# Opening of a two-layer diffusion step: a third input unit in PSUM banks of its own, its products spread between the modulation chunks

## What is computed

```python
def modulation(cond, w, b):
    m = jax.nn.silu(cond) @ w + b
    return m.reshape(cond.shape[0], 1, N_MOD, D_MODEL)

def modulate_in(x, g_pre, mod, j):
    return rmsnorm(x, g_pre) * (1.0 + mod[:, :, 3 * j + 1]) + mod[:, :, 3 * j]

def swiglu(h, w13, w2):
    a, g = jnp.split(h @ w13, 2, axis=-1)
    return (jax.nn.silu(g) * a) @ w2
```

## Time and profile before

| | us |
|---|---|
| runs | 2427.45, 2427.62, 2428.94 (median 2427.62) |
| the profiled execution | 2429.22 |
| its span | 2427.4 |
| busy: PE, DVE, ACT, POOL | 2392.8 (99%), 1747.2, 981.5, 435.0 |
| PE busy from 20 to 30, 30 to 40, 40 to 50 us | 5.09, 8.06, 8.86 |
| PE busy from 50 to 60, 60 to 70 us | 9.88, 10.00 |

### The profile page before, as it was taken

The page is one execution under the profiler, slowest core; times in us unless marked ns, Lnnn a source line. Parts: engine busy times, 40 slices in busy tenths (PEclk is TensorE's granted clock), DMA queues, the critical chain, the costliest instruction groups (busy, mean ns, idle before and its releaser), DMA issues. The chain is left out here.

```text
span 2427.4 us, 38749 instructions
## 1 busy us (share of the span) xinstructions
PE 2392.8 (99%) x15053; PEld 2196.1 (90%) x15053; DVE 1747.2 (72%) x2469; ACT 981.5 (40%) x1917; POOL 435.0 (18%) x462
## 2 busy tenths in 40 slices
PE   7999999999999999999999999999999999999998
PEld 6998999899889799979988997999899989989997
DVE  5988786566554779778846978885677769856863
ACT  4442343533445455324434442453511154423432
POOL 2220121211114223102213210220300021201211
PEclk9999999999999999999999999999999999999999
DMA  7526333385122453353253426334254433243333
GB/s 232 164 62 217 96 87 117 117 265 161 50 60 74 116 176 87 126 162 87 79 182 108 120 70 230 92 87 133 69 165 151 128 122 96 62 148 96 88 115 112
DMA packets 347227, 297.94 MB, mean 123 GB/s; under 512 B 38798, under 2 KB 296838, under 8 KB 347046
## 3 DMA queue, kind: packets, MB, share of 16 engines
q1 hardware_dynamic: 341798, 278.64, 38.1%
q0 software_dynamic: 5248, 16.83, 1.9%
HBM read 280.57 MB, written 14.80 MB: 122 GB/s over the span
## 5 line engine op out<-in xcount | busy, mean ns | idle before, releaser
L2071 DVE TENSOR_TENSOR w_lo<-w_raw,w_hi 128x512 fp32r<-128x512 f32 (+1 forms) x243 | 204.5, 845 | 225.4 <-ACT w_hi L1456 224.2
L1456 ACT ACTIVATE w_hi<-w_raw 128x512 fp32r<-128x512 f32 (+1 forms) x243 | 181.5, 752 | 445.2 <-DMA w_raw<-in_ffn_w_dram 202.5
L942 PE MATMUL psum<-w_hi,act_hi 128*128 128x512 f32 x800 | 318.3, 398 | 0.4 <-DVE w_lo L2071 0.4
L944 PE MATMUL psum<-w_hi,act_lo 128*128 128x512 f32 x800 | 317.1, 396 | 0.0
L943 PE MATMUL psum<-w_lo,act_hi 128*128 128x512 f32 x800 | 317.0, 396 | 0.0
L1080 PE MATMUL psum<-hT_hi,w_hi 128*128 128x320 f32 x912 | 281.9, 309 | 0.9 <-DVE z_quarters L2376 0.9
L1081 PE MATMUL psum<-hT_lo,w_hi 128*128 128x320 f32 x912 | 281.8, 309 | 0.0
L1082 PE MATMUL psum<-hT_hi,w_lo 128*128 128x320 f32 x912 | 281.8, 309 | 0.0
L1977 POOL TENSOR_TENSOR w_sum<-w_raw 128x512 f32<-128x512 f32 x36 | 54.8, 1523 | 744.0 <-DVE w_lo L2338 744.0
L1080 PE MATMUL psum<-t_hi,w_hi_more 128*128 128x320 f32 x608 | 187.9, 309 | 0.0
L1082 PE MATMUL psum<-t_hi,w_lo_more 128*128 128x320 f32 x608 | 187.9, 309 | 0.0
(11 more groups left out here) (319 smaller groups left out, 6003.1 us busy)
## 6 DMA issues: line engine op xcount, KB each, us to landing
w_raw<-in_ffn_w_dram SPq DMA_DIRECT2D x92, 512.0 KB, 5.1
w_raw_next<-in_ffn_w_dram SPq DMA_DIRECT2D x80, 512.0 KB, 5.3
w_raw<-in_ffn_w_dram SPq DMA_DIRECT2D x148, 256.0 KB, 3.2
ada_tile_ffn<-in_ada_w_dram SPq DMA_DIRECT2D x56, 512.0 KB, 4.1
ada_direct<-in_ada_w_dram POOLq DMA_DIRECT2D x32, 512.0 KB, 6.0
w_raw<-in_ab_w_in_dram SPq DMA_DIRECT2D x27, 512.0 KB, 4.0
ada_tile_sc<-in_ada_w_dram SPq DMA_DIRECT2D x24, 512.0 KB, 3.7
w_raw<-in_sc_w_in_dram SPq DMA_DIRECT2D x23, 512.0 KB, 4.0
```

The source lines that it names most:

```text
L942: mm(out, a_hi, b_hi, start=first, stop=False)
L944: return mm(out, a_lo, b_hi, start=False, stop=final)
L1456: A(dst, src, ACT.Copy).then_inc(w_hi_ok, 1)
L2071: V.tensor_tensor(d_, a, b.bitcast(F32), ALU.subtract).then_inc(w_lo_ok, 1)
```

## The change

The third unit (unit 2) gets banks 6 and 7; the columns of the modulation move from bank 7 into the upper half of banks 4 and 5. Unit 2's block is requested behind the second chunk. Its split stands ahead of chunk 1's rows on ACT and DVE. PE's order is rewritten, the opening doing all three units. DVE and ACT take the k steps one at a time. Behind the opening, DVE's split of unit 3 stands ahead of the split of u, and POOL's two sums wait for `w_lo_ok` 4 in the first sublayer, the low part of unit 3.

```diff
         THIRD = pair(6)
+        FIRST_COLS = 256
...
+                if c_ == 1:
+                    dma(next_raw[:], ffn_w13[0, 0].rearrange("(k p) n -> p k n", p=P)[:, :, FF + P:FF + 2 * P]).then_inc(next_loaded, 16)
-            dma(next_raw[:], ffn_w13[0, 0].rearrange("(k p) n -> p k n", p=P)[:, :, FF + P:FF + 2 * P]).then_inc(next_loaded, 16)
...
-                    last = nc.tensor.transpose(PS[:, 7, col:col + 2], mrow0[:, c_, i, :], ident[0:2, 0:2])
+                    last = nc.tensor.transpose(PS[:, 4 + c_ % 2, col:col + 2], mrow0[:, c_, i, :], ident[0:2, 0:2])
...
-                    for k in range(CK):
-                        for r in range(2):
-                            products(r, k)
-                    for c_ in range(1, CHUNKS):
-                        first_modulation(c_)
-                        if c_ == 1:
-                            first_columns(1)
-                            continue
-                        for j in range(CK):
-                            for r in range(2):
-                                products(r, (c_ - 1) * CK + j)
-                            if j == 0:
-                                first_columns(c_)
+                    both(0)
+                    both(1)
+                    first_modulation(1)
+                    products(2, 0)
+                    first_columns(1)
+                    products(2, 1)
+                    first_modulation(2)
+                    both(2)
+                    first_columns(2)
+                    both(3)
+                    first_modulation(3)
+                    products(0, 4)
+                    first_columns(3)
+                    products(1, 4)
+                    both(5)
+                    products(2, 2)
                     for r in range(2):
                         for k in range(KD - CK, KD):
                             products(r, k)
+                    for k in range(3, KD):
+                        products(2, k)
...   direct_step
-                    if s > 1:
+                    if s != 1:
                         pe.wait_ge(in_evac[UB[s] % 2], inv(plan[s][0], UB[s]) + 1)
...   the loop over units behind the opening
-                            for r in range(1 if s and i == 1 else 0, 2):
+                            for r in range(1 if i == 1 else 0, 2):
...   ACT, opening: split of unit 1 between k 0 and 1, unit 2 behind k 1
+                    modulate_first(c_ * CK)
+                    if c_ == 0:
+                        split(plan[0][0]["nin"] + 1)
+                    modulate_first(c_ * CK + 1)
+                    if c_ == 0:
+                        act.wait_ge(next_loaded, 16)
+                        A(next_hi[:], next_raw[:], ACT.Copy).then_inc(w_hi_ok, 1)
...   POOL
-                    pool.wait_ge(w_lo_ok, plan[s][0]["nin"] + 3)
+                    pool.wait_ge(w_lo_ok, plan[s][0]["nin"] + (3 if s else 4))
...   DVE, opening
+                first_rows(0)
+                first_cols(0)
+                split(n)
+                split_first(0)
+                split(n + 1)
+                split_first(1)
+                dve.wait_ge(w_hi_ok, n + 3)
                 V.tensor_tensor(next_lo[:], next_raw[:], next_hi[:].bitcast(F32), ALU.subtract).then_inc(w_lo_ok, 1)
+                first_rows(1)
+                first_cols(1)
+                split_first(2)
+                first_rows(2)
+                split_first(3)
+                first_cols(2)
+                split_first(4)
+                first_rows(3)
+                split_first(5)
+                first_cols(3)
+                split_first(6)
+                split_first(7)
...   DVE, mixed_in
-                    if i and not (s and i == 1):
+                    if i > 1:
                         split(nb + 1 + 2 * i)
...
-                    if s and i == 0 and ph["plain"]:
+                    if i == 0 and ph["plain"]:
                         split(nb + 3)
                     split_act(i, act_hi[:, i, :], act_lo[:, i, :], ut[:])
```

More of the change, by code:

```diff
@@ L920, in first_columns @@
                 for i in range(2 * CK):
-                    col = (i // CK * KD + c_ * CK + i % CK) * 2
-                    last = nc.tensor.transpose(PS[:, 7, col:col + 2], mrow0[:, c_, i, :], ident[0:2, 0:2])
+                    col = FIRST_COLS + (i // CK * KD + c_ * CK + i % CK) * 2
+                    last = nc.tensor.transpose(PS[:, 4 + c_ % 2, col:col + 2], mrow0[:, c_, i, :], ident[0:2, 0:2])
                 last.then_inc(mod_mm, 1)
@@ L982, in products, with both @@
                             pe.wait_ge(w_lo_ok, n + 1)
-                        for a, b in ((w_hi, hT_hi), (w_hi, hT_lo), (w_lo, hT_hi)):
+                        hi, lo = (next_hi, next_lo) if r == 2 else (w_hi[:, n % 2], w_lo[:, n % 2])
+                        out = THIRD if r == 2 else IN[n % 2]
+                        for a, b in ((hi, hT_hi), (hi, hT_lo), (lo, hT_hi)):
                             for h in range(2):
-                                last = mm(IN[n % 2][:, h, 0:HT], a[:, n % 2, k, :], b[:, k, h * HT:(h + 1) * HT],
-                                          start=(k == 0 and a is w_hi and b is hT_hi), stop=(k == KD - 1 and a is w_lo))
+                                last = mm(out[:, h, 0:HT], a[:, k, :], b[:, k, h * HT:(h + 1) * HT],
+                                          start=(k == 0 and a is hi and b is hT_hi), stop=(k == KD - 1 and a is lo))
                         if k == KD - 1:
                             last.then_inc(pe_unit, 1)
-                    for k in range(CK):
-                        for r in range(2):
-                            products(r, k)
-                    for c_ in range(1, CHUNKS):
-                        first_modulation(c_)
-                        if c_ == 1:
-                            first_columns(1)
-                            continue
-                        for j in range(CK):
-                            for r in range(2):
-                                products(r, (c_ - 1) * CK + j)
-                            if j == 0:
-                                first_columns(c_)
+                    def both(k):
+                        products(0, k)
+                        products(1, k)
+                    both(0)
[14 more added lines that the diff above has]
+                    products(2, 2)
                     for r in range(2):
@@ L1030, in in_unit @@
                 for k in range(KD):
-                    hi, lo = (next_hi[:, k, :], next_lo[:, k, :]) if ph["nin"] == 0 and first(r) and i == 1 else (w_hi[:, p, k, 0:width], w_lo[:, p, k, 0:width])
+                    hi, lo = w_hi[:, p, k, 0:width], w_lo[:, p, k, 0:width]
                     for a, b in ((hi, hT_hi), (hi, hT_lo), (lo, hT_hi)):
@@ L1514, in opening, with modulate_first @@
                     A(h_mod[:, :, q * P:(q + 1) * P], TR(0, q), ACT.Copy).then_inc(kept_by_act, 1)
+                def modulate_first(k):
+                    for cd, tok in ((0, slice(0, LAT)), (1, slice(LAT, TOK))):
+                        last = A(h_mod[:, k, tok], h_mod[:, k, tok], ACT.Identity, scale=mcol[:, 0, 1, cd, k:k + 1], bias=mcol[:, 0, 0, cd, k:k + 1])
+                    last.then_inc(first_hmod, 1)
                 for c_ in range(CHUNKS):
@@ L1520, in opening @@
                         split(plan[0][0]["nin"])
-                        split(plan[0][0]["nin"] + 1)
                         act.wait_ge(x_kept_dve, 3)
@@ L1658, in mixed_in @@
                     need(act, in_evac[(nb + 1) % 2], inv(ph, nb + 1) - 1 + i)
-                    A(halves(sg[:]), THIRD_V if s and i == 1 else IN_V[nb % 2], ACT.Silu).then_inc(in_evac[nb % 2], 1)
+                    A(halves(sg[:]), THIRD_V if i == 1 else IN_V[nb % 2], ACT.Silu).then_inc(in_evac[nb % 2], 1)
                     if i == 1:
@@ L2150, in evac, with split_first @@
                     V.tensor_copy(dst, src).then_inc(out_evac, 1)
[L2152 to L2157, removed]
+            def split_first(k):
+                dve.wait_ge(first_hmod, k + 1)
+                own.link(V.tensor_copy(hT_hi[:, k, :], h_mod[:, k, :]))
+                V.tensor_tensor(hT_lo[:, k, :], h_mod[:, k, :], hT_hi[:, k, :].bitcast(F32), ALU.subtract).then_inc(first_hT, 1)
             def opening():
@@ L2174, in opening, with first_rows @@
                 n = plan[0][0]["nin"]
[L2175 to L2178, removed]
+                def first_rows(c_):
                     dve.wait_ge(mod_mm, 2 * c_ + 1)
@@ L2181, in opening, with first_cols @@
                         V.tensor_copy(mrow0[:, c_, i, :], PS[32 * i:32 * i + 2, 4 + c_ % 2, 0:P]).then_inc(first_row, 1)
+                def first_cols(c_):
+                    ks = slice(c_ * CK, (c_ + 1) * CK)
                     dve.wait_ge(mod_mm, 2 * c_ + 2)
-                    turned_ = PS[:, 7, 0:4 * KD].rearrange("p (a k c) -> p a k c", a=2, c=2)
+                    turned_ = PS[:, 4 + c_ % 2, FIRST_COLS:FIRST_COLS + 4 * KD].rearrange("p (a k c) -> p a k c", a=2, c=2)
```

(6 more changed lines are left out.)

## The result

| | us |
|---|---|
| before, 21 runs | 2428.94 median (2427.08 to 2431.61) |
| changed, 21 runs | 2432.94 median (2430.97 to 2437.87) |
| ratio | 1.0018, 95% interval 1.0012 to 1.0024 (+2.9 to +5.8 us) |
| changed again, beside other kernels | 1.0013 (1.0004 to 1.0022), twice |
| profiled execution of the changed kernel | 2431.89, span 2430.1 |

One of the 33 runs of the kernel before that stand beside the first four experiments took 4005.03 us at a mean granted clock of 0.616, against 0.997 to 0.999 in the others; it is left out everywhere.

A forecast was written before the change was run, and what follows sets the result against it. PE was taken as the bound, busy 2392.8 of 2427.4 us. The opening's 3.3 us gain is eaten by the wait for POOL's direct loads, net +1.0 on 2427.62: 2428.6 us, range 2424.0 to 2432.2.

The forecast's parts named there:

- POOL's gate: POOL's sums start 3.6 us later, so the direct loads land late; PE stands some 4 us, unit 4 +1.0 us.
- the delay of POOL: POOL's sums beside DVE's copy and subtraction of u: delay bounded by 0 and 1.3 us, taken as 0.
- the clock: PE's new stand from 64.4 is broken by the direct steps, longest piece about 1.9 us: no fall forecast.
- the base: The kernel before's median, 2427.62 us, onto which the forecast difference was put.
- The loads, the start, unit 1's end: Opening: unit 2's block at 30.0, chunk 2 at 36.0, chunk 3 at 42.0; first pair done 0.65 us earlier.
- PE at unit 3 3.3 us earlier: Five k steps of unit 2 remain after the first pair, ending at 57.3 instead of 60.61.
- the cover of other steps: DVE's later work, such as unit 4's `w_lo` at 67.5, ends before PE needs it at 71.1: hidden.
- The 72.4: Start of unit 4 in us if DVE goes first with both its operations, blocking POOL.
- Rival B: Clock falls in PE's stand at the direct steps: 2.9 to 3.4 us on top of +1.0, 2431.8 us; chance 12%.
- Rival A: The gain stays: direct loads land before PE waits much, unit 4 at 66.8; -3.3 us, 2424.3 us; chance 20%.
- Rival C: Opening does not shrink, unit 2's early split standing ahead of chunk 1's rows; +1.6 us, 2429.2 us; chance 8%.
- Its sign: Rival C's mark in the profile: the last product of unit 1 not before 53.6 us.

The follow-up runs named there:

- the first four experiments: Four of the follow-up runs, timed beside 33 runs of the kernel before; the text does not say which four.
- filled: Changed kernel plus 14 further matmuls ahead of the first direct step, filling PE's wait; run twice, 2433.16 and 2433.47 us, ratio 1.0015 to before.
- gate 4 alone: Kernel before with only POOL's two sums in the first sublayer moved to wait for unit 3's low part; 2432.63 us, ratio 1.0013.
- early loads: Changed kernel, bias and first four direct loads issued after four k steps of h, sums gated by unit 2's low part; 2426.95 and 2428.75 us, 0.9991.
- gate 3: Changed kernel with POOL's sums waiting for unit 2's low part again, as before; 2428.72 us, ratio 0.9998 to before.

## Why the prediction was wrong

The measured 2432.94 lies above its time (2428.6) by 4.3 us and above its range (to 2432.2) by 0.7. The prediction took 4.9 us as about what a measurement can tell here; with 21 runs a side the interval is +2.9 to +5.8 us, so a loss of 4 us is clear of noise. The mechanism that decides, POOL's gate, was right; the steps that failed are the delay of POOL, the clock and the base, all put too low. Of the 4.3 us the base is 1.3, unit 4's start 0.6, the clock behind it 0.7, and 1.7 do not show in the profiles. Point by point, against the mean of two profiles of before and three of the changed kernel:

- *The loads, the start, unit 1's end.* Modulation 3 was forecast at 42.0 and came at 43.06, 42.52 and 42.67, as PE was bound by modulation 2's load (36.4 to 37.0, forecast 36.0) and then by its own work. Unit 1 was to end 0.65 us earlier; it ended 0.5 earlier by u's start (53.9 against 54.4). Right, though the 1.23 us gap ahead of k 2 was overlooked.
- *PE at unit 3 3.3 us earlier.* 58.1 against 61.25: 3.15. Right.
- *POOL's gate.* The mechanism, the order of waits and the cover of other steps were right: sums 2.6 us behind u's start, the first load 7.3 behind the sums, the last landing 7.8 behind that. The step that was mis-sized is "I bound the delay of POOL by 0 and 1.3 us and take 0": beside DVE's copy and subtraction of u the two sums took 6.58 instead of 6.13 us, against 5.89 with the gate alone, where DVE had done both before they began. Unit 4 was +1.6 instead of +1.0. In the prediction's own measure, from unit 1's end to unit 4, it is 18.4, 18.8 and 18.8 us instead of 18.0: 0.45 are POOL's sums, and 0.4 in the last two the last direct step at half clock. The 72.4 that the prediction gives for POOL late by 1.3 us is where unit 4 started, by coincidence: POOL was late by 0.45, and unit 1 ended at 54.00 in that profile, not at 52.9.
- *The clock.* "I forecast no fall" failed: it fell in all three profiles. Rival B had the mechanism (12%) and the wrong price, 2.9 to 3.4 us; the runs show 0, 0.8 and 1.3 us between unit 4 and the pairs, since most of the slow stretch lies where PE waits for loads anyway, and up to 0.4 in the last direct step. With it the pairs were +2.3 in the mean.
- *The level.* The sum was put on a median of 3 runs, 2427.62; 21 runs of before gave 2428.94. With +2.3 on that the time is 2431.2, within the range. A range on the absolute time has to carry the uncertainty of the base.
- *What is open.* The timed loss, 3.2 us in the mean of three comparisons (4.0, 2.5, 3.05), is 0.9 us more than the profiles' +2.3. It does not lie behind the pairs: there the profiles of both kernels have 2341.1 us in the mean. The other variants differ the same way: filled 3.5 timed and 1.3 in profiles, gate 4 alone 2.9 and 2.0, early loads -2.0 and -3.5. A profile is one execution. Those of the changed kernel were 0.6 us faster than the medians of their runs, those of before 0.5 us slower, and this alone is 1.1 us. What the other executions lose, and where, no profile shows.
- *Rival A* would have been nearer had the gate not been moved, but not right: with gate 3 unit 4 starts 1.8 us earlier than before, not 3.3. Only with early loads is it 3.5. *Rival C* is out: unit 2's early split was done on DVE (at 33.1 in the first profile) before modulation 1 ended on PE (33.7), so it did not hold the rows of chunk 1. Its sign, unit 1 not done before 53.6, is met in the first profile (54.00), and its +1.6 at unit 4 is the measured figure, both by coincidence: the sign stood against one early profile of before, and the +1.6 came with a unit 1 that ended 0.5 us earlier.

## What to carry to other kernels

A change that gets an engine somewhere earlier is worth what the next thing it waits for allows: follow the queue of the engine that issues that thing (here POOL: gate, two sums, bias, four loads) before adding up the filled gaps. A gate moved to spare one held instruction (here 1.6 us of DVE, off the path, and another was held for 2.6 instead) moves everything behind it in that queue. Issue loads that need no result of the gated work ahead of the gate.

## What the runs showed of the hardware that was not expected

The clock also falls where PE counts as busy throughout. PE's window of the kernel before, in the mixer, and the same of the first kernel with early loads:

```profile
580.00:585.00 5.00, 5.00 (x25) 0.66 0.28 73
```
```profile
580.00:585.00 5.00, 5.00 (x44) 1.00 0.13 27
```

The first is before, the second the other. The same code stands 2.9 us earlier there (the product behind the small matmuls starts at 577.60, in before at 580.46), and its clock is 1.00 in every microsecond from 572 to 592. What PE did ahead of the fall, from the timeline of before, is 28 matmuls of 4 to 10 columns in 2.2 us. The last group is

```profile
579.50 1.03 PE L1312 MATMUL psum<-m_prev,sel 4*128 4x10 f32 x8
```

The fall at this place is in 8 of the 13 profiles and not in the other 5 (the changed kernel's second, both filled kernels, gate 3, the first early loads), and PE counts as busy all the while. That the small matmuls are its cause was not tested.

The span behind the pairs' start is 2341.1 to 2344.5 us in the 8 profiles with the fall (2341.2 and 2341.1 in those of before) and 2339.6, 2339.6, 2341.0, 2341.1 and 2341.7 in the 5 without it. So the fall is at most one part of the spread. The 2344.5 is the second run of early loads, which has the fall, 1.4 us more of idle PE between 825 and 835 us than the first, and a lower clock (0.67) from 835 to 840. That is a spread of 5 us that does not follow the change, of the size of what was to be measured.
